# Block inverses with 32x32 weights in the RWKV part, and weights loaded in 512 KB halves

## The chip, the core and the metric

The kernel runs on one core of one Trainium2 chip. Its metric is the device time of one execution in microseconds (us), the median of three runs. It holds three transformer-like blocks behind one another, in float32, for 256 tokens of width 2048 (batch 1).

## The reference, cut to what matters

Nearly all arithmetic is the product of 256 tokens with large weight matrices. The part of the change that touches arithmetic lies in the first block, in the RWKV-7 mixer, whose recurrence over 256 positions is this (16 heads of 64):

```python
def step(state, inp):
    rt, wt, kt, vt, kkt, at = inp
    sa = jnp.einsum('bhvk,bhk->bhv', state, -kkt)
    state = (state * wt[:, :, None, :] + sa[..., None] * (kkt * at)[:, :, None, :]
             + vt[..., :, None] * kt[..., None, :])
    yt = jnp.einsum('bhvk,bhk->bhv', state, rt)
    return state, yt
...
_, y = lax.scan(step, state0, seq_major)
```

The projections around it are plain products, the three blocks run one behind the other:

```python
h = _rms_norm(x, pre_norm_g[l])
proj = h @ w_in[l]
...
merged = (jax.nn.sigmoid(m_r + b_merge[l, 0]) * u_r + jax.nn.sigmoid(m_a + b_merge[l, 1]) * u_a)
x = x + _rms_norm(merged @ w_out[l], post_norm_g[l])
```

## The kernel before, in words

**The bulk.** All weight matrices are streamed once from HBM, in units of 1 MB (128 partitions x 8 chunks x 256 columns of float32), into `ring`, a ring of three units (`RING = 3`). Half a unit is a slot (`SLOT = 4` chunks). ScalarE rounds a slot to its high part (`split_high`, L2700), VectorE computes the low part (`split_low`, L2707), and TensorE multiplies: high weights with both parts of the tokens (L2847, 512 columns move) and low weights with the high part of the tokens (L2851, 256 columns move), 8 products of each in a slot. One slot takes about 3 us, and there are 1084 slots. The parts of the weights lie in four buffers (`PARTS = 4`), so ScalarE and VectorE can be two slots ahead.

**The loads.** SyncE issues them in `load_unit`: for unit u it waits until `low_split` has counted both slots of unit u - 3, then issues one DMA of 1 MB, whose landing is counted by `unit_loaded[u % 3]`. Only the very first unit is loaded in two halves. ScalarE waits for the whole unit before it splits its first slot.

**The side work.** Norms, attention, the recurrence and so on are threads: generators for each engine that yield places on the axis of slots. Each engine walks along the slots and runs whatever of a thread is due before the next piece of bulk work. The places are written by hand, partly in a table `MOVED`, and every engine executes in order. So each engine's sequence is fixed when the program is built.

**The inverse.** The recurrence is computed in chunks of 64 positions, four at a time for a pair of heads. There are four rounds (i = 0 to 3), and in each round two such pairs, here called the even and the odd one (`rw` in the code; the even one's tiles lie in `high`, the odd one's partly in `low`). Every chunk needs the inverse of a triangular 64x64 matrix. It is built by doubling: `x0` is the inverse of the diagonal blocks of 2, and level l (1 to 5) joins the diagonal blocks of width 2^l to blocks of twice the width. `xx[:, 0]` and `xx[:, 1]` hold the inverse so far and its transpose, `al` the part of the matrix that level l needs (POOL masks it, L1086). A level has two steps on TensorE:

- step y: 8 products for each pair, with weights from `al` and 32 moving columns from `xx`. ScalarE then copies the result to `yb` (L1241).
- step xx: 16 products for each pair (8 in level 5), with weights from `xx` and `yb`, after ScalarE's copy. VectorE then adds the result to `xx` (L1165, L1169).

The two heads of a pair sit on partitions 0 to 63 and 64 to 127, and so every product uses a 64x64 quarter of the array. Every float32 product shows in the trace as two loads of weights and two matmuls. All these products have the line of the helper `mm` (L1285), and they go by their tiles: `sidep` is where they write.

In the program TensorE has, for each level, step y of the even pair, step y of the odd pair, then step xx of both. In 12 of the 16 levels 2 to 5 (four rounds of four levels) no bulk product stands between y and xx; in the other four (levels 2, 4 and 5 of round 0, level 4 of round 2) 8 or more bulk products do.

Of the kernel before, what the change touches and what calls it, by code (L numbers as in the profile page):

```python
# [22 lines left out]
RING = 3  # L23
# [170 lines left out]
def build_kernel(nc, I, out_dram):  # L194
    ctx = ExitStack()
    with ctx:
# [3 lines left out]
        def sem(name):  # L200
            return ctx.enter_context(nc.semaphore(name))
# [4 lines left out]
        ring = sb("ring", [P, RING, UNIT, NB])  # L206
# [18 lines left out]
        gp = ctx.enter_context(nc.psum_tensor("gp", [P, 2, 2, 2, TOK], F32))  # L225
        sp_ = ctx.enter_context(nc.psum_tensor("sidep", [P, 4, 512], F32))

        unit_loaded = [sem(f"unit_loaded_{k}") for k in range(RING)]
        high_split, low_split, slot_used = sem("high_split"), sem("low_split"), sem("slot_used")
        lo_copied, block_evacuated = sem("lo_copied"), sem("block_evacuated")  # L230
        scaled_by_vector, scaled_by_pool = sem("scaled_by_vector"), sem("scaled_by_pool")
# [46 lines left out]
        S, order = {}, []  # L278
# [37 lines left out]
        n_slots = order[-1].end  # L316
        where = [(s, b, n) for s in order for b in range(s.blocks) for n in range(s.slots)]
# [37 lines left out]
        rows, row_list = {}, []  # L355
# [509 lines left out]
        v1 = high[:, 4096:6144].rearrange("p (t c) -> p t c", t=2)  # L865
# [121 lines left out]
        def block_columns(a, l, u):  # L987

            return a.rearrange("p c (b u w) -> p c b u w", u=2, w=1 << l)[:, :, :, u, :]
# [290 lines left out]
        def rwkv_tensor(pe):  # L1280
            HS = [slice(0, 64), slice(64, 128)]
            ACROSS = [(HS[0], HS[1]), (HS[1], HS[0])]

            def mm(out, lhs, rhs, start=True, stop=True):
                return pe.matmul(out, lhs, rhs, start=start, stop=stop, skip_group_check=True)  # L1285

            def crossed(rw, n):

                return HS[n ^ rw.th], HS[n]
# [16 lines left out]
            for i in range(4):  # L1306
# [9 lines left out]
                for rw in rwkv:  # L1316
# [5 lines left out]
                    for t in range(2):  # L1322
                        m = mm(rw.x[:, t * P:(t + 1) * P], t1[0:65, t * P:(t + 1) * P], w2p[0:65, j * P:(j + 1) * P])
# [57 lines left out]
                for l in range(1, 6):  # L1381
                    t = t0 + 14 + 4 * (l - 1)
                    yield t
                    for rw in rwkv:
                        if l == 1:
                            rw.ac.wait(pe, "bonus", i)
                        rw.po.wait(pe, f"al{l}", i)
                        rw.dv.wait(pe, "x0" if l == 1 else f"xx{l - 1}", i)
                        for c in range(4):
                            for s, o in ACROSS:  # L1390
                                m = mm(rw.x[o, c * 32:(c + 1) * 32], rw.al[s, l % 2, c, :], block_columns(rw.xx[s, 1], l, 0)[:, c])
                        rw.pe_.did(m, f"y{l}")
                    yield t + 2
                    for rw in rwkv:
                        rw.ac.wait(pe, f"y{l}", i)
                        for c in range(4):
                            if l < 5:
                                for s, o in ACROSS:
                                    mm(rw.yk[s, c * 32:(c + 1) * 32], rw.xx[o, 0, c, :], block_columns(rw.yb[o], l, 0)[:, c])
                            for s, o in ACROSS:  # L1400
                                m = mm(rw.x[o, 256 + c * 32:256 + (c + 1) * 32], rw.yb[o, c, :], block_columns(rw.xx[o, 0], l, 1)[:, c])
                        rw.pe_.did(m, f"xx{l}")
                for c in range(4):
                    t = t0 + 34 + 6 * c
# [1255 lines left out]

        loads_of_unit = []
        for u in range(n_slots // 2):
            s, b, n = where[2 * u]
            loads_of_unit.append((loads_of_unit[u - RING] if u >= RING else 0) + 16 * len(s.source(b, n // 2)))

        def load_unit(sp, u):
            s, b, n = where[2 * u]
            if u >= RING:  # L2670
                sp.wait_ge(low_split, 2 * (u - RING) + 2)
            for src, c0, width in s.source(b, n // 2):
                to = ring[:, u % RING].rearrange("p (c x) n -> p c (x n)", x=2) if s.wide else ring[:, u % RING, :, c0:c0 + width]
                sp.dma_start(to, src).then_inc(unit_loaded[u % RING], 16)

        first_half_loaded = sem("first_half_loaded")

        def load_half(sp, half):
            (src, _, _), = S["v1"].source(0, 0)
            to = ring[:, 0].rearrange("p (c x) n -> p c (x n)", x=2)  # L2680
            return sp.dma_start(to[:, 2 * half:2 * half + 2], src[:, 2 * half:2 * half + 2])

        def load_first_half(sp):
            load_half(sp, 0).then_inc(first_half_loaded, 16)

        def load_second_half(sp):
            load_half(sp, 1).then_inc(unit_loaded[0], 16)

        def split_high(act, q):
            if q >= n_slots:  # L2690
                return
            s, b, n = where[q]
            u = q // 2
            if q == 0:
                act.wait_ge(first_half_loaded, 16)
            else:
                act.wait_ge(unit_loaded[u % RING], loads_of_unit[u])
            if q >= PARTS:
                act.wait_ge(slot_used, q - PARTS + 1)
            act.activation(w_parts[:, q % PARTS, 0], ring[:, u % RING, SLOT * (q % 2):SLOT * (q % 2) + SLOT, :], ACT.Copy).then_inc(high_split, 1)  # L2700
# [241 lines left out]
```

## Time and profile before

| | |
|---|---|
| median of three runs | 3282.01 us (3281.84 to 3282.38) |
| the profiled execution | 3281.76 us, of which 3280.0 us span |
| TensorE busy (matmuls) | 3260.6 us, 99% of the span |
| weight loads of TensorE | 2829.2 us, 86% |
| VectorE, ScalarE, GpSimd | 2131.2, 1510.4, 359.0 us |
| granted TensorE clock | 0.999 |
| DMA | 181 GB/s in the mean, 55.3% of the 16 engines' span for the weights' queue |

How to read it: the span runs from the first to the last instruction; the execution's own time has 1.8 us around it. Busy time counts an engine's instructions. Matmuls overlap, so that TensorE's pace is read better from the distance between the starts of its instructions. The rows further down give a start, a length, an engine, the line of the kernel, out<-in by the names of the program, the shape, and how many instructions are merged into the row. A gap before an instruction is given in brackets with what ended it.

### The profile page before, as it was taken

Reading aid. Unit: us, or ns where it says so; the run is one execution under the profiler, and the core shown is the slowest. Engines: PE = TensorE matmul, PEld = TensorE weight load, DVE = VectorE, ACT = ScalarE, POOL = GpSimd, SP = SyncE. Lnnn points to the kernel's source line nnn. Section 1 sums busy time; section 2 is a strip of 40 time slices with the busy share of each in tenths; the row PEclk is TensorE's granted clock in tenths of the full one; section 3 lists DMA queues with packets and bytes.
Section 4 is the critical chain, followed back from the end, with each engine's and each line's share of the span. In section 5 each row is a group of like instructions: output and inputs, shape, how many; then the busy total and the mean of one; then the engine's idle time right before and its main releaser. Section 6 shows DMA issues by size and latency. Waiting matters only on the chain.

```text
span 3280.0 us, 50954 instructions
## 1 busy us (share of the span) xinstructions
PE 3260.6 (99%) x21299; PEld 2829.2 (86%) x21299; DVE 2131.2 (65%) x2795; ACT 1510.4 (46%) x2049; POOL 359.0 (11%) x356
## 2 busy tenths in 40 slices
PE   9999999999999999999999999999999999999999
PEld 8888888888878888888888888888888888888887
DVE  6468666567487677776765556656778765456654
ACT  5355434444544455445444444444455544334443
POOL 3000233310102004211000000012000100000000
PEclk9999999999999999999999999999999999999999
DMA  7455434456546456555556556555555555556554
GB/s 252 148 181 179 146 128 131 133 171 225 182 145 204 161 180 231 169 180 194 190 182 204 189 177 198 194 171 197 182 171 168 190 186 201 193 182 197 197 193 154
DMA packets 533065, 594.98 MB, mean 181 GB/s; under 512 B 16773, under 2 KB 475365, under 8 KB 532326
## 3 DMA queue, kind: packets, MB, share of 16 engines
q1 hardware_dynamic: 532694, 591.48, 55.3%
q8 instruction: 169, 2.77, 0.3%
q14 instruction: 58, 0.48, 0.0%
q10 hardware_dynamic: 144, 0.26, 0.0%
HBM read 585.32 MB, written 6.32 MB: 180 GB/s over the span
## 4 chain that ended last, share of the span: by engine, by line
PE 97%; DVE 2%; ACT 0%; POOL 0%; issue 0%; DMA 0%; SPq 0%; POOLq 0%; ACTq 0%; DVEq 0%
PE gp L2847 49%; PE gp L2851 26%; PE gp L2767 10%; PE gp L2773 5%; PE sidep L1285 3%; DVE w_parts L2707 1%; PE sidep L1571 0%; PE sidep L1575 0%; PE sidep L1853 0%; DMA high<-x 0%; PE sidep L1991 0%; PE sidep L833 0%; PE sidep L834 0%; DVE x_parts L2550 0%; PE sidep L960 0%
## 5 line engine op out<-in xcount | busy, mean ns | idle before, releaser
L2707 DVE TENSOR_TENSOR w_parts<-ring,w_parts 128x1024 fp32r<-128x1024 f32 x1084 | 1369.7, 1286 | 384.2 <-ACT w_parts L2700 382.0
L2700 ACT ACTIVATE w_parts<-ring 128x1024 fp32r<-128x1024 f32 x1084 | 1108.9, 1052 | 460.8 <-PE gp L2773 230.0
L2847 PE MATMUL gp<-x_parts,w_parts 128*128 128x512 f32 x5264 | 1296.6, 394 | 0.0
L2847 PEld LDWEIGHTS gp<-x_parts,w_parts 128*128 128x128 f32 x5264 | 958.9, 188 | 186.1 <-issue 2.5
L2851 PEld LDWEIGHTS gp<-x_parts,w_parts 128*128 128x128 f32 x5264 | 684.2, 191 | 34.5 <-issue 2.5
L2851 PE MATMUL gp<-x_parts,w_parts 128*128 128x256 f32 x5264 | 706.2, 284 | 0.4 <-DVE w_parts L2707 0.4
L2243 ACT ACTIVATE lo_half<-gp 128x512 f32<-128x512 f32 x220 | 131.6, 598 | 726.6 <-PE gp L2847 593.7
L2847 PE MATMUL gp<-ff_parts,w_parts 128*128 128x512 f32 x1792 | 430.4, 391 | 0.0
L2847 PEld LDWEIGHTS gp<-ff_parts,w_parts 128*128 128x128 f32 x1792 | 328.9, 188 | 63.3
L2372 DVE TENSOR_TENSOR stage<-gp,lo_half 128x512 f32<-128x512 f32 x168 | 116.0, 690 | 311.7 <-ACT lo_half L2243 309.7
L2767 PE MATMUL gp<-w_parts,ff_parts 128*128 128x512 f32 x1024 | 273.7, 389 | 0.0
L2851 PEld LDWEIGHTS gp<-ff_parts,w_parts 128*128 128x128 f32 x1792 | 231.1, 191 | 10.4 <-issue 1.0
L2851 PE MATMUL gp<-ff_parts,w_parts 128*128 128x256 f32 x1792 | 235.9, 283 | 0.0
L2767 PEld LDWEIGHTS gp<-w_parts,ff_parts 128*128 128x128 f32 x1024 | 192.2, 188 | 39.8
L658 POOL TENSOR_TENSOR low<-low 128x512 f32<-128x512 f32 (+1 forms) x38 | 59.7, 1577 | 1126.0 <-ACT low L649 655.3
L2773 PE MATMUL gp<-w_parts,ff_parts 128*128 128x512 f32 x512 | 157.6, 389 | 0.0
L2767 PE MATMUL gp<-w_parts,x_parts 128*128 128x512 f32 x512 | 140.4, 396 | 0.2 <-ACT w_parts L2700 0.2
L2259 ACT ACTIVATE ff_parts<-stage 128x512 fp32r<-128x512 f32 x64 | 40.5, 632 | 166.9 <-DVE stage L2409 166.9
L2773 PEld LDWEIGHTS gp<-w_parts,ff_parts 128*128 128x128 f32 x512 | 96.1, 188 | 20.0
L2767 PEld LDWEIGHTS gp<-w_parts,x_parts 128*128 128x128 f32 x512 | 94.8, 188 | 20.0 <-issue 0.4
L2372 DVE TENSOR_TENSOR high<-gp,lo_half 128x512 f32<-128x512 f32 x45 | 31.1, 690 | 109.9 <-ACT lo_half L2243 109.9
L2291 POOL TENSOR_TENSOR high<-high,rstd 128x512 f32<-128x512 f32 x26 | 46.6, 1796 | 340.2 <-DVE high L2372 340.2
(376 smaller groups left out, 2007.9 us busy)
## 6 DMA issues: line engine op xcount, KB each, us to landing
ring<-w_in SPq DMA_DIRECT2D x219, 1024.0 KB, 5.1
ring<-w_ff SPq DMA_DIRECT2D x128, 1024.0 KB, 5.6
ring<-w_up SPq DMA_DIRECT2D x64, 1024.0 KB, 5.8
ring<-w_down SPq DMA_DIRECT2D x64, 1024.0 KB, 4.9
ring<-w_out SPq DMA_DIRECT2D x48, 1024.0 KB, 5.5
ring<-w_branch_attn SPq DMA_DIRECT2D x8, 1024.0 KB, 6.0
ring<-w_branch_rwkv SPq DMA_DIRECT2D x8, 1024.0 KB, 5.7
gate_scratch<-stage SPq DMA_DIRECT2D x16, 256.0 KB, 2.2
```

Source lines behind the costliest of these rows:

```text
L658: m = pool.tensor_tensor(self.acc[k], self.acc[k], self.sq[b - 1][k], ALU.add)
L1285: return pe.matmul(out, lhs, rhs, start=start, stop=stop, skip_group_check=True)
L2243: act.activation(lo_half[:, k % 2], gp[:, k % 2, :, 1, :], ACT.Copy).then_inc(lo_copied, 1)
L2259: act.activation(ff_parts[:, 2 * b:2 * b + 2, 0, :], st, ACT.Copy).then_inc(ff_high_split, 1)
L2291: pool.tensor_tensor(to, to, over(rstd, 2), ALU.mult).then_inc(scaled_by_pool, 1)
L2372: v.tensor_tensor(to, gp[:, k % 2, :, 0, :], lo_half[:, k % 2], ALU.add).then_inc(block_evacuated, 1)
L2700: act.activation(w_parts[:, q % PARTS, 0], ring[:, u % RING, SLOT * (q % 2):SLOT * (q % 2) + SLOT, :], ACT.Copy).then_inc(high_split, 1)
L2707: v.tensor_tensor(w_parts[:, q % PARTS, 1], ring[:, u % RING, SLOT * (q % 2):SLOT * (q % 2) + SLOT, :], w_parts[:, q % PARTS, 0].bitcast(F ...
L2767: pe.matmul(wide_sums(k, t), operand(s, b, s.chunks * n + c)[:, half, tokens], w[:, 0, c, :], start=(n == 0 and c == 0 and half == 0), sto ...
L2773: m = pe.matmul(wide_sums(k, t), operand(s, b, s.chunks * n + c)[:, 0, tokens], w[:, 1, c, :], start=False, stop=(n == s.slots - 1 and c = ...
L2847: return pe.matmul(gp[:, k % 2, j, :, :], w_parts[:, q % PARTS, 0, c, j * P:(j + 1) * P], operand(s, b, SLOT * n + c), start=(n == 0 and c ...
L2851: return pe.matmul(gp[:, k % 2, j, 0, :], w_parts[:, q % PARTS, 1, c, j * P:(j + 1) * P], operand(s, b, SLOT * n + c)[:, 0, :], start=Fals ...
```

## The change

Four things are edited.

1. In levels 2 to 4, step y works on 32x32 blocks: for each chunk and each head two products with 32x32 weights and 16 moving columns instead of one with 64x64 weights and 32 moving columns. Level 1 is as before.
2. In level 5, step y has products with 32x32 weights (one quarter of `al`) and 32 moving columns, as many products as before.
3. In level 5, step xx does the same with a quarter of `yb` as weights.
4. Every unit is loaded by two DMAs of 512 KB, one for each slot. The first waits until `low_split` has counted one slot of unit u - 3, the second until it has counted both. Each half has its own semaphore for each place of the ring, and ScalarE waits for the half that it splits.

```diff
-                            for s, o in ACROSS:
-                                m = mm(rw.x[o, c * 32:(c + 1) * 32], rw.al[s, l % 2, c, :], block_columns(rw.xx[s, 1], l, 0)[:, c])
+                            if l == 1:
+                                for s, o in ACROSS:
+                                    m = mm(rw.x[o, c * 32:(c + 1) * 32], rw.al[s, l % 2, c, :], block_columns(rw.xx[s, 1], l, 0)[:, c])
+                            elif l < 5:
+                                for b in range(2):
+                                    for s, o in ACROSS:
+                                        m = mm(rw.x[half(o, b), c * 32 + b * 16:c * 32 + (b + 1) * 16],
+                                               rw.al[half(s, b), l % 2, c, b * 32:(b + 1) * 32],
+                                               block_columns(rw.xx[half(s, b), 1, :, b * 32:(b + 1) * 32], l, 0)[:, c])
+                            else:
+                                for s, o in ACROSS:
+                                    m = mm(rw.x[half(o, 1), c * 32:(c + 1) * 32], rw.al[half(s, 0), l % 2, c, 32:64],
+                                           rw.xx[half(s, 0), 1, c, 0:32])
...
-                                m = mm(rw.x[o, 256 + c * 32:256 + (c + 1) * 32], rw.yb[o, c, :], block_columns(rw.xx[o, 0], l, 1)[:, c])
+                                if l < 5:
+                                    m = mm(rw.x[o, 256 + c * 32:256 + (c + 1) * 32], rw.yb[o, c, :], block_columns(rw.xx[o, 0], l, 1)[:, c])
+                                else:
+                                    m = mm(rw.x[half(o, 0), 256 + c * 32:256 + (c + 1) * 32], rw.yb[half(o, 1), c, 0:32],
+                                           rw.xx[half(o, 1), 0, c, 32:64])
...
-            if u >= RING:
-                sp.wait_ge(low_split, 2 * (u - RING) + 2)
-            for src, c0, width in s.source(b, n // 2):
-                to = ring[:, u % RING].rearrange("p (c x) n -> p c (x n)", x=2) if s.wide else ring[:, u % RING, :, c0:c0 + width]
-                sp.dma_start(to, src).then_inc(unit_loaded[u % RING], 16)
+        def load_half(sp, u, half):
...
+            rows = slice(half * s.chunks, (half + 1) * s.chunks)
+            if u >= RING:
+                sp.wait_ge(low_split, 2 * (u - RING) + 1 + half)
+            sp.dma_start(to[:, rows], src[:, rows]).then_inc(half_loaded[u % RING][half], 16)
...
-            if q == 0:
-                act.wait_ge(first_half_loaded, 16)
-            else:
-                act.wait_ge(unit_loaded[u % RING], loads_of_unit[u])
+            act.wait_ge(half_loaded[u % RING][q % 2], 16 * (u // RING + 1))
```

On TensorE, in round 0, the products of level 3 with what stands around them, before (the first row is bulk; 64x32 means 64 partitions and 32 moving columns):

```order
L2851 MATMUL gp<-x_parts,w_parts 128x256 x8
L1285 MATMUL sidep<-high 64x32 x8
L1285 MATMUL sidep<-low 64x32 x8
L1285 MATMUL sidep<-high 64x32 x16
L1285 MATMUL sidep<-high,low 64x32 x2
L1285 MATMUL sidep<-low,high 64x32 x2
```

and the same place of the changed kernel (its L2859 is L2851 of before):

```order
L2859 MATMUL gp<-x_parts,w_parts 128x256 x8
L1285 MATMUL sidep<-high 32x16 x16
L1285 MATMUL sidep<-low 32x16 x16
L1285 MATMUL sidep<-high 64x32 x16
L1285 MATMUL sidep<-high,low 64x32 x2
L1285 MATMUL sidep<-low,high 64x32 x2
```

The two y rows have twice the products, each a quarter as large in weights; the xx rows and all places are the same.

On SyncE, the first loads of the ring and the loads behind the parameters, before:

```order
L2674 DMA ring<-w_in 128x4x512
L431 DMA high<-x 128x2x1024
L2674 DMA ring<-w_in 128x4x512
...
L2674 DMA ring<-w_in 128x4x512 x5
L2674 DMA ring<-w_in 128x8x256 x2
```

and of the changed kernel:

```order
L2688 DMA ring<-w_in 128x2x512 x2
L431 DMA high<-x 128x2x1024
L2688 DMA ring<-w_in 128x2x512 x2
...
L2688 DMA ring<-w_in 128x2x512 x10
L2688 DMA ring<-w_in 128x4x256 x4
```

Every load of a unit has become two with half the rows, at the same place of the queue; no other DMA has moved past one.

## Rows read from the trace of the kernel before

**Rows 1.** The page: busy time by engine (instructions), the last chain by engine.

```profile
PE 3260.6 (99%) x21299; PEld 2829.2 (86%) x21299; DVE 2131.2 (65%) x2795; ACT 1510.4 (46%) x2049; POOL 359.0 (11%) x356
...
PE 97%; DVE 2%; ACT 0%; POOL 0%; issue 0%; DMA 0%; SPq 0%; POOLq 0%; ACTq 0%; DVEq 0%
```

**Rows 2.** Busy time by stretch: stretch, length, PE, PEld, DVE, ACT, POOL, clock, DMA, GB/s.

```profile
460.00:540.00 80.00, 78.85 (x1223) 67.28 (x1222) 48.03 (x94) 31.52 (x61) 29.14 (x27) 1.00 0.39 127
```

**Rows 3.** Groups by form, 380 to 710 us: count, busy us, mean ns, idle before.

```profile
L1285 PEld LDWEIGHTS sidep<-high 64*64 64x64 f32 x1696 | 46.3, 134 | 19.7 <-issue 12.7 <-DVE high L1188 1.6 <-DVE high L1145 0.4
L1285 PE MATMUL sidep<-high 64*64 64x32 f32 x896 | 26.5, 222 | 0.0
...
L1285 PEld LDWEIGHTS sidep<-headones,high 128*128 128x128 f32 x56 | 6.8, 191 | 0.8 <-ACT high L1257 0.6
```

**Rows 4.** Order of time on PE, round 1, level 3, nothing between y and xx.

```profile
491.31 0.66 PE L1285 MATMUL sidep<-high 64*64 64x32 f32 x16
491.79 0.63 PE L1285 MATMUL sidep<-low 64*64 64x32 f32 x16
492.34 0.67 PE L1285 MATMUL sidep<-high 64*64 64x32 f32 x32
...
493.25 0.23 PE L1285 MATMUL sidep<-low,high 64*64 64x32 f32 x2
493.40 2.11 PE L2847 MATMUL gp<-x_parts,w_parts 128*128 128x512 f32 x8
```

**Rows 5.** Order of time on ScalarE at the same place.

```profile
492.01 0.28 ACT L1241 ACTIVATE high<-sidep 128x128 f32<-128x128 f32 x1 [3.41 <-PE sidep L1285]
492.48 0.28 ACT L1241 ACTIVATE high<-sidep 128x128 f32<-128x128 f32 x1 [0.19 <-PE sidep L1285]
```

**Rows 6.** PE, round 0, level 2, where bulk stands behind y.

```profile
405.04 0.66 PE L1285 MATMUL sidep<-high 64*64 64x32 f32 x16
405.52 0.63 PE L1285 MATMUL sidep<-low 64*64 64x32 f32 x16
406.09 2.11 PE L2847 MATMUL gp<-x_parts,w_parts 128*128 128x512 f32 x8
```

**Rows 7.** PE, round 1, level 5.

```profile
504.28 0.65 PE L1285 MATMUL sidep<-high 64*64 64x32 f32 x16
504.76 0.63 PE L1285 MATMUL sidep<-low 64*64 64x32 f32 x16
505.31 0.66 PE L1285 MATMUL sidep<-high 64*64 64x32 f32 x16
505.80 0.63 PE L1285 MATMUL sidep<-low,high 64*64 64x32 f32 x16
506.36 0.97 PE L2847 MATMUL gp<-x_parts,w_parts 128*128 128x512 f32 x3
```

**Rows 8.** PE, round 1, level 2, the second y step.

```profile
485.83 0.28 PE L1285 MATMUL sidep<-low 64*64 64x32 f32 x3
486.78 0.48 PE L1285 MATMUL sidep<-low 64*64 64x32 f32 x11 [0.68 <-issue]
```

**Rows 9.** The page's DMA queues: packets, MB, share.

```profile
q8 instruction: 169, 2.77, 0.3%
```

**Rows 10.** ScalarE's waits for loads, in all: us, times, longest.

```profile
ACT w_parts L2700 <- DMA ring<-w_in: 3.2, 3, 1.8
ACT w_parts L2700 <- DMA ring<-w_ff: 2.2, 1, 2.2
ACT w_parts L2700 <- DMA ring<-w_branch_rwkv: 2.2, 1, 2.2
```

**Rows 11.** TensorE's waits at the same splits, and SyncE's for a free place.

```profile
PE gp L2767 <- ACT w_parts L2700: 0.2, 1, 0.2
...
SPq L2674 <- DVE w_parts L2707: 2830.7, 528, 19.6
```

**Rows 12.** Loads of the ring from `w_in`: count, KB, median us to landing.

```profile
ring<-w_in SPq DMA_DIRECT2D x219, 1024.0 KB, 5.1
```

More of the change, by code:

```diff
@@ L226, in build_kernel @@
         sp_ = ctx.enter_context(nc.psum_tensor("sidep", [P, 4, 512], F32))
-        unit_loaded = [sem(f"unit_loaded_{k}") for k in range(RING)]
+        half_loaded = [[sem(f"half_loaded_{k}_{half}") for half in range(2)] for k in range(RING)]
         high_split, low_split, slot_used = sem("high_split"), sem("low_split"), sem("slot_used")
@@ L1285, in mm, with half @@
                 return pe.matmul(out, lhs, rhs, start=start, stop=stop, skip_group_check=True)
+            def half(s, b):
+                return slice(s.start + 32 * b, s.start + 32 * b + 32)
             def crossed(rw, n):
@@ L2658, in operand @@
             return x_parts[:, c]
-        loads_of_unit = []
-        for u in range(n_slots // 2):
+        def load_half(sp, u, half):
             s, b, n = where[2 * u]
-            loads_of_unit.append((loads_of_unit[u - RING] if u >= RING else 0) + 16 * len(s.source(b, n // 2)))
-        def load_unit(sp, u):
-            s, b, n = where[2 * u]
-            if u >= RING:
-                sp.wait_ge(low_split, 2 * (u - RING) + 2)
-            for src, c0, width in s.source(b, n // 2):
-                to = ring[:, u % RING].rearrange("p (c x) n -> p c (x n)", x=2) if s.wide else ring[:, u % RING, :, c0:c0 + width]
-                sp.dma_start(to, src).then_inc(unit_loaded[u % RING], 16)
[L2676 to L2681, printed above, removed]
+            (src, c0, width), = s.source(b, n // 2)
+            to = ring[:, u % RING].rearrange("p (c x) n -> p c (x n)", x=2) if s.wide else ring[:, u % RING, :, c0:c0 + width]
+            rows = slice(half * s.chunks, (half + 1) * s.chunks)
+            if u >= RING:
+                sp.wait_ge(low_split, 2 * (u - RING) + 1 + half)
+            sp.dma_start(to[:, rows], src[:, rows]).then_inc(half_loaded[u % RING][half], 16)
+        def load_unit(sp, u):
+            load_half(sp, u, 0)
+            load_half(sp, u, 1)
         def load_first_half(sp):
-            load_half(sp, 0).then_inc(first_half_loaded, 16)
+            load_half(sp, 0, 0)
         def load_second_half(sp):
-            load_half(sp, 1).then_inc(unit_loaded[0], 16)
+            load_half(sp, 0, 1)
         def split_high(act, q):
```

## The prediction

> **What bounds the kernel now.** I read the page first. TensorE is busy for 3260.6 of 3280.0 us, its clock stays at the full level, and the last chain of waits is 97% TensorE [rows 1]. So time is won or lost only where TensorE's own stream becomes shorter or where TensorE stands still. The view by stretches then shows the part that holds the inverse, 380 to 700 us: TensorE has some 1220 matmuls in 80 us there, VectorE and ScalarE stand at 48 and 32 us of 80, and DMA at 0.39 [rows 2]. No other engine is near its limit in it. The groups by form show what is to be changed: 896 matmuls of 64x32 in one of four such groups, 1792 in all (112 products of levels 1 to 5 for each pair and round, 8 pairs and rounds, two records each), and weight loads of 64 columns with 134 ns against 191 ns with 128 columns [rows 3]. Last I read the order of time at single levels, since busy time of overlapping matmuls says little.
>
> **What one step costs.** In a step y 16 records take 0.48 us (491.31 to 491.79), and they go through two quarters of the array at once: 8 turns of 60 ns. In a step xx 64 records of both pairs take 1.06 us (492.34 to 493.40), of which 0.15 us is the change back to the whole array, so about 15 ns each: four quarters at once, again in turns of 60 ns [rows 4]. The length of a turn is thus set by one quarter's load of weights and matmul, not by how many quarters run. A load of 64 fewer columns is 57 ns shorter [rows 3], 0.89 ns for a column. With 32 columns a turn should be 28 ns shorter, and 8 turns 0.23 us. Since the first turn has a start-up that stays, I take 0.215 us for each changed step. Level 2 to 4 have twice the records in y, but four tiles of the array instead of two, and so 8 turns as well.
>
> The trace has no 32x32 product, so this has two ends. From below: a turn stays at 60 ns, and nothing is won. From above: it falls to what four records need if only their starting counts. The densest row has 15 ns for a record [rows 4], but that is a turn of 60 ns shared by four; it does not show that 15 ns is the least. I take 32 ns for a turn, as the weight loads of two widths lie on a line. I keep both ends.
>
> **The sum, part by part.**
>
> (a) Levels 2 to 4 without bulk between y and xx: 9 of them (of the 12 such levels, 3 are level 5). Here ScalarE's copy decides when xx may start. The even y begins at 491.31, ScalarE's copy at 492.01 and ends at 492.29, xx begins at 492.34, 1.03 us after y [rows 4, 5]. TensorE's own work before xx, two steps y, will be 0.27 + 0.25 us, but the copy can come earlier only by what the even y becomes shorter. So xx starts at about 0.85 instead of 1.03 us, 0.18 us are won, and the rest of what y saves becomes a wait of TensorE. The odd pair's copy is ready at about 1.12, before xx of the even pair is through. 9 x 0.18 = 1.6 us.
>
> (b) Levels 2 to 4 with bulk behind y (3): y of both pairs was 0.48 + 0.57 us [rows 6], and the copy is hidden by the bulk. Both savings count: 3 x 0.43 = 1.3 us.
>
> (c) Level 5 without bulk between (3): 504.28 to 506.36 is 2.08 us [rows 7]. Now xx even starts at 0.85 and takes 0.27; the odd copy follows the even one (start 0.52, each 0.28 us [rows 5]) and lets xx odd start at 1.12; it then takes 0.56 - 0.215 = 0.35. End at 1.47: 3 x 0.6 = 1.8 us.
>
> (d) Level 5 with bulk between (1): four steps, 4 x 0.215 = 0.9 us.
>
> (e) The change between ways of dividing the array. From 64x64 back to the whole array it costs 0.15 us from the last start to the next (493.25 to 493.40) where a turn is 0.06 [rows 4]. The change adds none where y or level 5 borders on bulk. It adds one of 32x32 to 64x64 in each of the 9 levels of (a), between odd y (through at about 0.54) and xx (0.85): it lies inside the wait for the copy. I take 0; without that cover it is at most 9 x 0.15 = 1.35 us. The Trainium skill says the same more strictly (TensorEngine Tiling, Key Properties): changing the mode of tiling drains the engine, changing the tile does not. The trace agrees with its 0.15 us; by that rule with nothing hidden the sum would be 1.35 us smaller.
>
> (f) The gap at 485.9. In the odd y of level 2, round 1, the records stop for 0.95 us from the start of one row to the next, where three records take 0.09, with no semaphore waited for ("issue") [rows 8]. The page has a DMA queue that loads instructions, 169 packets with 2.77 MB, some 16 KB each [rows 9]; with 42,598 loads and matmuls [rows 1] that is about 65 bytes for an instruction, and 250 in a packet. My reading: TensorE had used up its instructions and waited 0.86 us for the next packet. Such a packet shares the DMA engines with a weight load, which is under way for 5.1 us of every 6 [rows 12]. Halves make these bursts shorter, and all positions move. I count 0.86 x 0.7 = 0.6 us as won.
>
> (g) The halves themselves. The first half of a unit may start one slot (3 us) earlier, and a half lands sooner. But in the whole program ScalarE waited only 7.6 us for a load in five places [rows 10], and TensorE 0.2 us for such a split [rows 11]: the two slots of lead cover the rest. SyncE waits 2830.7 us for places of the ring [rows 11], so 542 more issues (about 0.4 us each) lie in idle time. Behind the added wait for the first slot stands the wait for the second, which ends when it ended before, so no store or side load comes later. I take 0. The bounds: +0.3 us if some side load is late, -0.5 if the first units help.
>
> Sum: 1.6 + 1.3 + 1.8 + 0.9 + 0.6 = 6.2 us. 3281.76 - 6.2 = 3275.6 for an execution like the profiled one, which lies 0.25 us under the median of the runs: **3275.8 us**.
>
> Nothing else is uncovered by it: between xx of a level and y of the next stands bulk of 1 to 3 us, in which VectorE adds and POOL masks, and these move together with TensorE's stream.
>
> **The rivals.**
>
> *B, four 32x32 tiles do not run together.* For it: the trace never has more than two row groups, and no record pace under 15 ns [rows 4]. Against: the pairs of a turn start together, and xx runs four quarters. Then 32 records of y need 0.48 us as the 32 of an xx do, and (a) and (b) are worth nothing, while level 5 (two tiles at a time) keeps (c) and (d): 2.7 + 0.6 = 3.3 us, 3278.7. The Trainium skill has a rule for this (TensorEngine Tiling, Gotcha 1: PSUM Pressure): row tiles cannot write one bank of PSUM at the same time. All tiles of a step y write one bank. The trace does not bear it out for two row tiles, whose matmuls in y go in pairs.
>
> *C, a 32-column load is not shorter.* Then no step changes its time, and what remains is the 32-to-64 change, partly behind the copy: 9 x 0.08 (0.15 less the wait of 0.07 that is there now) = 0.7 slower: 3282.7. For it: nothing under 64 columns is in the trace. Against: the line through 134 and 191 ns.
>
> *D, slower: TensorE runs out of instructions more often.* The place is the run of y and xx: a level of (a) has 192 instructions in 2.1 us now and 256 in 1.9 us afterwards, a whole packet. Each gap costs 0.86 us [rows 8]. There was one in 16 levels. It takes 7 new ones to use up the 5.6 us of (a) to (d), from 8 on the kernel is slower; 14 would make it 3288. For it: the existing gap lies in just such a run. Against: one in 16, and shorter bursts of weight loads.
>
> *E, more is won:* steps and copies become shorter by what 32 rows and 16 columns save in a matmul's 219 to 222 ns [rows 3], 0.03 us in each of 16 levels and 12 copies, 0.8 us, and the gap of (f) goes for good: 3274.5.
>
> **How the numbers follow.** Forecast 0.58 (its own range 3275.0 to 3277.2), B 0.18, C 0.07, D 0.05, E 0.12. The range of 8 in 10 takes in E and B and leaves C and D out: 3274.2 to 3279.8. A difference of 0.2% is 6.6 us, about the least that a measurement of this kernel can tell from no change; that is 3275.4. E and somewhat under half of the forecast's share lie beyond it: faster 0.38, within 0.2% 0.57, slower 0.05 (D).
>
> **What the profile would show.** 32x32 weight loads of about 106 ns; in level 3 of round 1 0.27 us from even to odd y and xx 0.85 us after y, with a wait of TensorE for ScalarE before it; level 5 in 1.47 us; the row of 485.9 without its gap; bulk rows with the same pace. The forecast is wrong if the even y still takes 0.48 us (B or C), if rows with "issue" gaps multiply (D), or if the bulk's pace or TensorE's waits for `w_parts` move (g).

## The result: slower by 0.25%, not faster

| | before | after |
|---|---|---|
| median (range), 9 runs each | 3281.65 us (3280.59 to 3282.38) | **3289.87 us** (3285.02 to 3293.58) |
| the profiled execution, its span | 3281.76, 3280.0 us | 3288.11, 3286.4 us |
| mean granted clock | 0.999 | 0.997 |

The ratio is 1.0025 [1.0016, 1.0033]. The forecast was 3275.8 us with a range of 3274.2 to 3279.8, and 0.05 for slower: it was wrong, in sign too. The runs of after also scatter over 8.6 us, those of before over 1.8.

**The steps that were changed.** They came out as forecast. The groups by form of after, 380 to 710 us (columns as in [rows 3]):

```profile
L1285 PEld LDWEIGHTS sidep<-high 32*32 32x32 f32 x512 | 7.1, 112 | 4.3 <-issue 1.0 <-ACT high L1241 0.8 <-POOL high L1090 0.7
L1285 PE MATMUL sidep<-high 32*32 32x16 f32 x384 | 5.7, 186 | 0.0
```

A weight load of 32 columns takes 112 ns, where 64 take 134. Now TensorE in round 1, level 3, which answers to [rows 4]:

```profile
494.09 0.44 PE L1285 MATMUL sidep<-high 32*32 32x16 f32 x32
494.37 0.52 PE L1285 MATMUL sidep<-low 32*32 32x16 f32 x32
494.94 0.67 PE L1285 MATMUL sidep<-high 64*64 64x32 f32 x32
...
496.01 0.73 PE L2855 MATMUL gp<-x_parts,w_parts 128*128 128x512 f32 x2
```

and ScalarE there, which answers to [rows 5] (both copies merged into one row):

```profile
494.61 0.62 ACT L1241 ACTIVATE high<-sidep 128x128 f32<-128x128 f32 x2 [3.25 <-PE sidep L1285]
```

The even y takes 0.28 us for 32 matmuls (0.48 for 16 before), and xx starts 0.85 us after y instead of 1.03. Level 2 of round 0, with bulk behind y, answers to [rows 6]:

```profile
405.30 0.44 PE L1285 MATMUL sidep<-high 32*32 32x16 f32 x32
405.57 0.45 PE L1285 MATMUL sidep<-low 32*32 32x16 f32 x32
405.95 1.42 PE L2855 MATMUL gp<-x_parts,w_parts 128*128 128x512 f32 x5
```

0.65 us instead of 1.05. And level 5 of round 1, which answers to [rows 7]:

```profile
507.52 0.44 PE L1285 MATMUL sidep<-high 32*32 32x32 f32 x16
507.79 0.42 PE L1285 MATMUL sidep<-low 32*32 32x32 f32 x16
508.44 0.44 PE L1285 MATMUL sidep<-high 32*32 32x32 f32 x16 [0.23 <-ACT high L1241]
508.71 0.42 PE L1285 MATMUL sidep<-low,high 32*32 32x32 f32 x16
509.06 2.11 PE L2855 MATMUL gp<-x_parts,w_parts 128*128 128x512 f32 x8
```

1.54 us instead of 2.08 here, 1.44 in the other two.

**Where the time went.** TensorE's waits in after, whole program (engine, tile and line, releaser: total us, times, longest):

```profile
PE sidep L1285 <- issue: 5.6, 4, 1.8
...
PE gp L2855 <- issue: 0.5, 1, 0.5
```

An "issue" wait is one that nothing in the trace ends. Before had one of 0.7 us [rows 8]. The longest two, in TensorE's order of time (round 0, level 3, and round 3, level 2):

```profile
411.62 0.22 PE L1285 MATMUL sidep<-low,high 64*64 64x32 f32 x1
413.51 0.24 PE L1285 MATMUL sidep<-low,high 64*64 64x32 f32 x1 [1.67 <-issue]
...
414.10 2.08 PE L2855 MATMUL gp<-x_parts,w_parts 128*128 128x512 f32 x4
...
662.13 0.28 PE L1285 MATMUL sidep<-high,low 64*64 64x32 f32 x3
664.19 0.19 PE L1285 MATMUL sidep<-high,low 64*64 64x32 f32 x1 [1.78 <-issue]
```

In the middle of a step xx, whose line the change does not touch, TensorE stands still for 1.89 us from start to start, and nothing that it waits for is in the trace. The five gaps are, from start to start: 1.89 (411.6), 0.73 (489.1), 1.05 (503.7), 1.82 (579.5) and 2.00 us (662.2), 7.5 in all. The one at 489.1 is in the same step as the gap of before, the odd y of level 2, round 1:

```profile
488.90 0.34 PE L1285 MATMUL sidep<-low 32*32 32x16 f32 x19
489.79 0.30 PE L1285 MATMUL sidep<-low 32*32 32x16 f32 x13 [0.56 <-issue]
```

So the old gap did not go, and four came with the change.

The bulk row at 414.10 shows a second loss: four products take as long as eight do [rows 4]. The view by stretches, around the gaps (columns as in [rows 2]):

```profile
405.00:411.60 6.60, 6.48 (x247) 5.43 (x248) 2.15 (x5) 3.04 (x8) 2.26 (x4) 1.00 0.57 183
411.60:413.50 1.90, 0.23 (x16) 0.12 (x8) 0.55 (x2) 0.64 (x1) 0.59 (x1) 1.00 0.86 250
413.50:420.00 6.50, 6.49 (x134) 4.71 (x134) 1.68 (x3) 0.94 (x3) 0.00 (x0) 0.54 0.35 110
...
581.30:588.10 6.80, 6.80 (x139) 5.43 (x138) 1.70 (x5) 1.04 (x3) 3.40 (x4) 0.50 0.46 138
...
664.20:670.00 5.80, 5.68 (x152) 4.94 (x152) 2.22 (x6) 2.05 (x5) 2.64 (x4) 1.00 0.02 6
```

Before, during and behind the gap the granted clock is 1.00, 1.00 and 0.54: after 1.9 us with TensorE at 0.23 us busy it fell to its lower level of 1.2 GHz. The trace's clock records give 6.83 us at 0.5 here and again from 581.27, behind the gap of 579. Behind the gap of 662, which is longer, it stayed at 1.00. The Trainium skill has idle time of TensorE as the cause of such a fall (TensorE: Matmul & The Clock Gate, Part 1: The HAM clock gate); the rows at 411 and 579 agree, the one at 662 shows that the length of one gap does not settle it.

**The balance of the two spans.** Steps: 9 x 0.18 + 3 x 0.4 + 1.8 + 0.9 = 5.5 us won. New gaps: 7.5 less the 5 x 0.06 us that such records take anyway, less the old one, 0.86: +6.3. Clock: at half speed four products of 512 columns take 2.01 us from start to start (414.10 to 416.11) instead of 1.12 (412.43 to 413.55 in before), and a step y or xx about 1.5 to 1.7 times its time, so 6.83 us cost about 2.9: twice, +5.8. Sum +6.6; the spans differ by 6.4 (3286.4 - 3280.0).

**What the gaps have in common.** I numbered the records of TensorE in the trace, that is its entries: weight loads, matmuls and its own semaphore and drain entries. The 16 profiles have 39 such gaps, all between 400 and 670 us. In every one the first record behind it has the number 193 over a multiple of 256, and the packet of the instruction queue that began last before it is always the same one: with packets counted from 0, record 256k + 449 follows packet k. The page of after, answering to [rows 9]:

```profile
q8 instruction: 172, 2.82, 0.4%
```

So the instructions come in packets of 256 (16 KB of 64 bytes each), and the boundaries stand at fixed numbers. That gives the theory for the experiments: TensorE asks for a packet some 294 records before it needs it (near record 155 over a multiple of 256, by the packets that begin soonest), the packet begins 0.1 to 6.4 us later (after, 380 to 710 us), and its instructions can be used about 2.35 us after it began (2.2 to 2.8 over the 39 gaps; 411.10 to 413.51 in after, 484.35 to 486.78 before). Where 294 records take longer than both, nothing is seen. In bulk alone, with 32 records in a slot of 3 us, they take some 27 us. In a level without bulk 256 records take 1.9 us.

### The profile page after: what moved, and what is told of

The parts are those of the page before. It is cut to its first block, busy times and chain, and to the rows that moved or that the text cites. A ratio compares the mean times of both kernels' runs of the same rounds, so it can differ in the third digit from the quotient of the medians.

```text
span 3286.4 us, 52263 instructions
## 1 busy us (share of the span) xinstructions
PE 3260.2 (99%) x21683; PEld 2826.8 (86%) x21683; DVE 2131.5 (65%) x2795; ACT 1511.0 (46%) x2049; POOL 358.5 (11%) x356
## 3 DMA queue, kind: packets, MB, share of 16 engines
q8 instruction: 172, 2.82, 0.4%
## 4 chain that ended last, share of the span: by engine, by line
PE 96%; DVE 2%; ACT 1%; issue 1%; POOL 0%; DMA 0%; SPq 0%; POOLq 0%; ACTq 0%; DVEq 0%
PE gp L2855 49%; PE gp L2859 25%; PE gp L2775 10%; PE gp L2781 5%; PE sidep L1285 3%; DVE w_parts L2715 1%; PE sidep L1589 0%; PE sidep L1593 0%; DMA high<-x 0%; PE sidep L1871 0%; PE sidep L2009 0%; PE sidep L833 0%; PE sidep L834 0%; DVE x_parts L2568 0%; PE sidep L960 0%
## 5 line engine op out<-in xcount | busy, mean ns | idle before, releaser
L2859 PEld LDWEIGHTS gp<-x_parts,w_parts 128*128 128x128 f32 x5264 | 684.3, 191 | 34.4 <-issue 2.5
L2859 PE MATMUL gp<-x_parts,w_parts 128*128 128x256 f32 x5264 | 706.2, 284 | 0.4 <-DVE w_parts L2715 0.4
L2859 PEld LDWEIGHTS gp<-ff_parts,w_parts 128*128 128x128 f32 x1792 | 231.0, 191 | 10.4 <-issue 1.0
L2859 PE MATMUL gp<-ff_parts,w_parts 128*128 128x256 f32 x1792 | 235.9, 283 | 0.1
```

Source lines behind the costliest of these rows:

```text
L2859: return pe.matmul(gp[:, k % 2, j, 0, :], w_parts[:, q % PARTS, 1, c, j * P:(j + 1) * P], operand(s, b, SLOT * n + c)[:, 0, :], start=Fals ...
```

## The experiments

Sixteen levels have many chances to meet a boundary, and one added record moves all later ones. All runs below are timed in five rounds against before on the same chip (fill_192 and fill_256 on another chip than the rest); the medians of before were 3281.3 to 3281.6 us. The intervals of the ratios are about 0.1% (3 us) to either side, so that no time alone decides between runs less far apart; there the gaps in the traces have to carry the reading. "Gaps" are TensorE's "issue" gaps, from start to start, in the profiled execution; "half clock" is the time at 0.5 in its clock records, between 380 and 710 us.

| run | median (range) us | ratio to before | span | gaps, us | half clock |
|---|---|---|---|---|---|
| inverse_only | 3290.86 (3289.55-3295.28) | 1.0030 [1.0019, 1.0042] | 3292.7 | 2.82 0.99 2.37 3.37 | 23.9 |
| halves_only | 3280.98 (3280.28-3282.07) | 0.9998 [0.9989, 1.0007] | 3279.9 | 0.62 | 0 |
| level5_only | 3278.88 (3278.28-3279.39) | 0.9991 [0.9982, 1.0] | 3277.4 | 1.10 | 0 |
| level5_halves | 3278.78 (3277.95-3279.62) | 0.9990 [0.9982, 0.9999] | 3277.3 | 0.82 | 0 |
| one_block | 3276.32 (3275.20-3277.73) | 0.9985 [0.9977, 0.9994] | 3274.6 | 0.57 1.11 | 0 |
| twice_64 | 3296.42 (3296.03-3297.72) | 1.0047 [1.0033, 1.006] | 3294.7 | 0.59 0.77 1.50 | 3.4 |
| more_records | 3286.43 (3285.26-3289.64) | 1.0015 [1.0007, 1.0024] | 3285.8 | 0.43 2.77 | 6.8 |
| level5_fill | 3278.61 (3278.15-3279.00) | 0.9991 [0.9983, 1.0] | 3277.0 | 0.46 | 0 |
| even_only | 3285.41 (3282.96-3289.76) | 1.0014 [1.0005, 1.0023] | 3283.5 | 0.81 0.40 0.42 1.99 1.62 1.12 | 3.4 |
| split_only | 3286.30 (3281.60-3288.05) | 1.0012 [1.0003, 1.0021] | 3283.1 | 0.82 2.25 2.13 0.56 | 3.4 |
| change_fill | 3283.78 (3283.13-3286.07) | 1.0009 [1.0, 1.0017] | 3282.0 | 0.95 0.48 1.59 2.16 | 6.8 |
| even_fill | 3291.00 (3284.74-3293.00) | 1.0028 [1.0018, 1.0038] | 3290.3 | 2.14 2.22 | 23.9 |
| fill_192 | 3283.62 (3283.23-3284.87) | 1.0007 [0.9998, 1.0016] | 3281.8 | 1.02 | 0 |
| fill_256 | 3283.04 (3282.32-3283.75) | 1.0005 [0.9996, 1.0013] | 3281.4 | 0.88 | 0 |

### Which edit costs

**inverse_only** is the change with whole loads of 1 MB, **halves_only** the loads in halves with the inverse of before.

> The 32x32 products of levels 2 to 5 with whole 1 MB loads. Theory S (the denser bursts of instructions run TensorE out of instructions, whatever the loads are): three or more gaps without a semaphore in the levels of the inverse, the level steps themselves as short as in the changed kernel (y to xx 0.85 us, level 5 in 1.44 us), and a time of 3283 to 3292 us that varies by several us from run to run. Theory H (the halves delay the instruction packets, the products alone are harmless): at most one gap and 3275 to 3277 us, with runs within 1 us of each other.

> Only the loads in halves, the inverse with 64x64 products as before. Theory S: no more gaps than before (one, or none), 3281 to 3283 us. Theory H: two or more gaps and 3284 us or more, since two or three loads of 512 KB are now under way at once and an instruction packet waits behind them.

The loss is all with the inverse; the halves alone are within 0.03% of before (just under what was expected), and their one gap is that of before: theory H, that the halves delay the packets, is refuted. Without the halves the gaps are even longer, up to this one in TensorE's order of time:

```profile
665.54 0.28 PE L1285 MATMUL sidep<-high,low 64*64 64x32 f32 x3
668.96 0.19 PE L1285 MATMUL sidep<-high,low 64*64 64x32 f32 x1 [3.15 <-issue]
```

**level5_only** has the small products in level 5 alone, **level5_halves** also the halves. Neither adds a record. The edit against the change:

```diff
-                            if l == 1:
+                            if l < 5:
                                 for s, o in ACROSS:
                                     m = mm(rw.x[o, c * 32:(c + 1) * 32], rw.al[s, l % 2, c, :], ...
-                            elif l < 5:
-                                for b in range(2):
...
```

> 32x32 products in level 5 alone, with whole loads; the number of instructions is that of before. By the steps measured in the changed kernel each of three level 5 becomes 0.64 us shorter (2.08 to 1.44) and one 0.8 us: 2.7 us less, 3279.0 us, if no gap is added. Theory S: it stays so, as no burst has more instructions, though level 5 runs through its 128 instructions in less time; with one new gap 3280 to 3283 us. Theory H says the same of this kernel.

> 32x32 products in level 5 alone, with the loads in halves. Theory S: as with level 5 and whole loads, 3278 to 3280 us. Theory H: two or more gaps, 3282 us or more. If both theories hold a part (bursts and late packets together), this one lies with level 5 and whole loads, and the full change is the worst of all.

Both hit: 2.7 us are won, as (c) and (d) had it. One gap is left, at the same product as before ([rows 8]), here in level5_only:

```profile
484.88 0.28 PE L1285 MATMUL sidep<-low 64*64 64x32 f32 x3
486.04 0.48 PE L1285 MATMUL sidep<-low 64*64 64x32 f32 x11 [0.88 <-issue]
```

### More records, or faster ones

**one_block** leaves out the second 32x32 block of step y in levels 2 to 4 (with whole loads); so it has the small products, but as many records as before. Against the change:

```diff
                             elif l < 5:
-                                for b in range(2):
+                                for b in range(1):
```

> The 32x32 products with whole loads, but in levels 2 to 4 step y computes only the first of its two 32x32 blocks (the other block is left out). The records are as many as before the change, and the steps as short as in the change. Theory S with the count of instructions as the cause: at most one gap, the clock at its full level all the time, and about 3276 us (3281.6 less the 5.6 us that the steps were to give). Theory S with the density as the cause (more instructions for a time, whatever their count): three or more gaps, 3282 us or more.

3276.3 us, 5.1 under before: the steps' 5.5 us, less 0.8 for a second gap, within 0.4. Small and fast products alone bring no new long gap; they do bring a second short one (0.57 us, where at most one was expected), at a boundary that before crossed without a stop: the same records come faster.

**twice_64** has the large products of before, each of levels 2 to 4 twice: the records of the change.

```diff
-                            for s, o in ACROSS:
+                            for s, o in ACROSS * (2 if 1 < l < 5 else 1):
                                 m = mm(rw.x[o, c * 32:(c + 1) * 32], ...
```

> The kernel before, with every 64x64 product of step y issued twice in levels 2 to 4: as many records as in the change, at the pace of before. Each of the 24 steps y takes 0.48 us more, 11.5 us in all, less nothing, so 3293 us without gaps. Count as the cause: gaps at 411, 490 and 580 us too, since a level now has 256 instructions, but shorter ones than in the change by about the 0.96 us that a level is longer: 3293 to 3297 us. Density as the cause: no new gap, 3292.5 to 3293.5 us.

In its interval, but the gaps stand at 413.7, 662.5 and 666.7 us, and not at 490 and 580 as expected. Here the reading by the median misleads: of the 14.7 us more span most is the second y itself, and the gaps are only 2.9 us, where the change has 7.5. It does not tell the number from the place.

**more_records** is before with 32 small identity products near the start (at 10 us, four records each), where TensorE waits for its first data; **level5_fill** the same with 16 of them on level5_halves.

```diff
+                if g == 2:
+                    fill(pe, 32)
                 pe.wait_ge(x_loaded[(0, 1, 2, 2, 3, 3, 3, 3)[g]], 16)
```

> The kernel before, with 32 small 64x64 products of the identity at the start, where TensorE waits for the tokens anyway: 128 more records, none of them in the inverse. Theory P (instructions come in packets of 256, a late packet stops TensorE at a record whose number is 193 over a multiple of 256): the gap at 485.9 us goes, and gaps appear at other places of the program, again at such a number. By the time from the request of a packet (155 records over a multiple) to the last record that TensorE has, the tightest places are at 487, 578 and 650 us (3.9 to 4.0 us, against over 5.6 everywhere before); one to three gaps there, 3282 to 3285 us. Theory Q (the gap at 485.9 is a matter of that place in the program, such as its data or its DMA): the gap stays at that step, no other, and 3281.6 to 3282.5 us.

> 32x32 products in level 5, loads in halves, and 16 small products at the start (64 records), so that the packet that is late at 485 us is requested before the denser step. Theory P: no gap at 485, the tightest places 4.8 us at 401 and 478 us, which is enough for a packet that starts 1 to 2 us after its request; 3278.8 less 0.8 = 3278.0 us. Theory Q: the gap stays, 3278.8 us or a little more.

The inverse of more_records is that of before to the last instruction, and its long gap comes 640 us later than the added products, which cost 0.8 us themselves (the first bulk behind them starts at 11.49 us, before at 10.68). Yet it is 5 us slower. In its order of time, round 3, a step xx that had no gap before:

```profile
651.69 0.23 PE L1293 MATMUL sidep<-high,low 64*64 64x32 f32 x2
654.46 0.32 PE L1293 MATMUL sidep<-low,high 64*64 64x32 f32 x2 [2.55 <-issue]
```

64 records ahead (level5_fill) cost nothing, 128 cost 5 us. I had expected the gaps of more_records at 487, 578 and 650 and 3282 to 3285. Those at 578 (0.43 us) and 652 came, the one at 487 did not, and the time is over the interval, as the clock fell behind the long gap (6.83 us), which no expectation had counted.

### Half of the change, and other places

**even_only** has the 32x32 blocks of levels 2 to 4 in the even pair alone, since only its y decides when ScalarE may copy; **split_only** in the three levels with bulk behind y; both have level 5 as in the change, and whole loads. Each of the two lines is the condition of one run, named behind it:

```diff
-                            if l == 1:
+                            if l == 1 or l < 5 and rw is rwkv[1]:                   # even_only
+                            if l < 5 and (i, l) not in ((0, 2), (0, 4), (2, 4)):    # split_only
```

> Only the even pair's y of levels 2 to 4 has 32x32 blocks (level 5 as in the change, whole loads). The even y alone decides when ScalarE's copy may start, so (a) should be kept whole (1.6 us) and half of (b) (0.65 us), with half of the added records (384 instead of 768). Theory N (it is the number of records of TensorE that comes too fast for the packets, and each added one counts): level5_only's 3278.9 less 2.2, plus one gap or two of 0.5 to 2 us in place of the four: 3277 to 3281, point 3279; a mark of the theory is that every gap stands where the record's number is 193 over a multiple of 256. Rival G (gaps come only where a whole packet of 256 lies in one level without bulk, which 224 records don't reach): no new gap, 3276.6.

> 32x32 blocks only in the three levels (round 0 levels 2 and 4, round 2 level 4) in which bulk products stand between y and xx, and level 5 as in the change, whole loads. Step (b) forecasts 1.3 us for these three: level5_only's 3278.9 less 1.3 = 3277.6. The 192 added records stand where bulk gives the packets time, so theory N expects no gap of their own (they move later boundaries by 64 to 192 records, which may cost or give back one gap of 0.5 to 1 us): 3277 to 3278.6. If the mere presence of 32x32 blocks brought the gaps, 2 us or more would be added: 3279.6 or more.

Both fall outside their intervals, and split_only falsifies what I then held: it adds 192 records where bulk is near, was to win 1.3 us, and lost 7.4 against level5_only. Its two longest gaps are in a step xx of round 0 and in bulk of round 1, neither of which it edits:

```profile
416.48 0.28 PE L1285 MATMUL sidep<-high,low 64*64 64x32 f32 x4
418.80 0.30 PE L1285 MATMUL sidep<-low,high 64*64 64x32 f32 x4 [2.03 <-issue]
...
493.91 0.73 PE L2865 MATMUL gp<-x_parts,w_parts 128*128 128x512 f32 x2
496.38 1.22 PE L2865 MATMUL gp<-x_parts,w_parts 128*128 128x512 f32 x2 [1.74 <-issue]
```

**change_fill** is the whole change with 24 small products ahead (96 records), **even_fill** even_only with 16.

> The whole change, and 24 small identity products before it all (96 records, under 1 us, where TensorE waits for the first loads anyway). All later records move by 96 against the boundaries of the packets. If a gap depends on where a boundary falls, the gaps at 411.6 and 662 should change their places or lengths: the boundaries then fall at about 410, 416, 491, 495, 579 and 661. The time lies anywhere between 3283 and 3292, but the profile's gaps stand at other products than in the change. The densest spots (491 and 579) lie in runs of more than 256 records, so that no shift frees the change of its gaps: at least two are left. If a gap belongs to a product (a tile, a mode of the array) and not to a boundary, places and time stay as they are, 3289.9.

> even_only with 16 small identity products before it all (64 records). Against even_only it tells how much the place of the boundaries does at half of the added records: theory N expects the same number of gaps give or take one, at other places, 3276.6 to 3281; rival G the same as even_only, 3276.6.

With the same inverse and loads, 96 records ahead make the change 6 us faster, as expected with gaps at other products; 64 ahead make even_only 5.6 us slower, 10 us over the interval, with two long gaps in place of six gaps, and 23.9 us at half clock. change_fill's first gap stands in y of the next level instead of in xx:

```profile
413.53 0.32 PE L1293 MATMUL sidep<-low 32*32 32x16 f32 x16
414.62 0.31 PE L1293 MATMUL sidep<-low 32*32 32x16 f32 x16 [0.77 <-issue]
```

No theory in which a record has a price explains both signs. Left is the place of the boundaries.

### The decisive pair

**fill_192** and **fill_256** are more_records with 48 and 64 products. 256 records bring every boundary back to its old product.

> The kernel before with 64 small identity products in front (256 records). Theory Z (what counts is where the boundaries of the packets of 256 records fall in the stretches without bulk, not how many records there are): 256 records bring every later boundary back to the product at which it stood before. The inverse then has the one gap of before, again in the odd y of level 2 of round 1, and none like the 2.8 us at 652 that 128 records brought. The products themselves delay the start: 128 of them took 0.8 us of TensorE's first bulk, 256 should take 2.0 us. So 3281.5 + 2.0 = 3283.5, 3282.5 to 3284. Rival C (each added record costs by its number): twice the loss of 128 records, 3281.5 + 10 = 3291.

> The same with 48 products (192 records), which cost 1.4 us at the start. Theory Z: the boundaries fall inside runs without bulk at about 487 and 578 (the 294 records from a packet's request to the first of the next take 4.1 to 4.2 us there, where 2.4 us and a packet's delay of 2 to 4 us are needed), so one or two gaps of 0.5 to 2 us at those places, each at a record whose number is 193 over a multiple of 256: 3281.5 - 0.8 + 1.4 + 1 to 5 = 3283 to 3287, point 3284.5. Rival C: between 128 and 256 records, 3289.

fill_256 hit: 3283.04, although it has twice the added records of more_records. The gap is back at its old product, after the third matmul of the odd y of level 2, round 1 ([rows 8]):

```profile
487.20 0.28 PE L1293 MATMUL sidep<-low 64*64 64x32 f32 x3
488.14 0.48 PE L1293 MATMUL sidep<-low 64*64 64x32 f32 x11 [0.66 <-issue]
```

The count up to it, by stretches, first in before and then in fill_256 (columns as in [rows 2]):

```profile
0.00:486.50 486.50, 481.00 (x3869) 414.84 (x3870) 317.37 (x499) 221.84 (x356) 90.51 (x128) 1.00 0.53 174
```

```profile
0.00:487.90 487.90, 483.39 (x3997) 417.60 (x3998) 317.28 (x499) 222.10 (x356) 90.49 (x128) 1.00 0.53 173
```

128 matmuls and 128 loads more, the same product, the same gap. fill_192 has its one gap at 577.9, one of the two places that the spacing of records had named, and its time is in the interval, 0.9 us under the point. That time has some luck in it: besides the gap of 1.02 us, TensorE waits 0.97 us at 967 us for a small side DMA, which no theory had named:

```profile
967.15 2.00 PE L1664 MATMUL sidep<-high 64*128 64x256 f32 x16 [0.97 <-DMA high<-high]
```

The pair also answers another rival, that the added products act by moving TensorE in time against the loads: fill_192 and more_records start the bulk at the same time (0.82 and 0.81 us later than before), and yet they have different gaps and times 2.8 us apart. (The fills cost less than I took: 1.35 us for 256 records, 0.82 for 192, by the start of the first bulk behind them.)

**What adds up and what doesn't.** Take before's span, less the steps (5.5, or the part of them that a run has), plus the start of the fill, plus gaps (less 0.06 each and the old 0.84), plus 0.42 us for each us at half clock (2.9 / 6.83). inverse_only: 3280.0 - 5.5 + 9.3 - 0.84 + 10.0 = 3293.0, measured 3292.7. more_records: 3280.0 + 0.8 + 3.1 - 0.84 + 2.9 = 3286.0, measured 3285.8. fill_256: 3280.0 + 1.35 + 0.82 - 0.84 = 3281.3, measured 3281.4. change_fill: 3280.0 - 5.5 + 0.7 + 4.9 - 0.84 + 2.9 = 3282.2, measured 3282.0 (the 0.7 is from the fills of 64 and 128 records, 0.57 and 0.8). In fill_192, split_only and even_only the sum is 0.9, 1.0 and 1.8 us too low. In fill_192 it is the wait for the side DMA shown above, in split_only the same wait (0.90 us at 968). In even_only 1.1 us of it are the steps themselves, which give less there. Round 2, level 2:

```profile
575.91 0.44 PE L1285 MATMUL sidep<-high 32*32 32x16 f32 x32
576.28 0.65 PE L1285 MATMUL sidep<-low 64*64 64x32 f32 x16
```

Where 64x64 products follow at once, the even y takes 0.37 us until the next start instead of 0.27: the change from 32x32 to 64x64 costs 0.10 us when no wait hides it. Each of the 12 levels then wins 0.09 us, where the expectation had 0.18 to 0.22. About 0.7 us stay unexplained.

The best versions with the whole computation are level5_fill and level5_halves, 3278.6 and 3278.8 us: 2.8 us, 0.09%, under before (the intervals end at 1.0000 and 0.9999), and 11 us under the change. Two runs that differ by so little are not told apart.

## Why the prediction was wrong

- **(a) to (d), right.** 0.18 us in a level without bulk, 0.40 of 0.43 with bulk, level 5 in 1.44 to 1.54 us for 1.47, and 0.84 of 0.86 in the level 5 of round 0. Medians confirm the sum: level5_only won 2.7 us of 2.7, one_block 5.1 of 5.6, and its second gap takes 0.8 of that.
- **Rivals B and C, refuted.** 32 matmuls in 0.28 us, in four tiles at once, and loads of 112 ns. The rule that the Trainium skill has on one bank of PSUM (TensorEngine Tiling, Gotcha 1: PSUM Pressure), and that B leaned on, does not show in either step y: each writes one bank, from two rows of tiles before and from four in the change, and its turns take 60 and 32 ns.
- **(e), right.** Between odd y and xx TensorE waits for ScalarE in any case, and xx starts at 0.85 us. The change of mode is hidden; even_only shows it uncovered, at 0.10 us, not 0.15.
- **(g), right.** halves_only: 0.9998. ScalarE waits 1.6 us for loads in after instead of 7.6, and TensorE gains nothing.
- **(f) and rival D: the steps that failed.** (f) read the gap of 485.9 rightly, as a packet of instructions that came late, and then treated it as an accident of 0.86 us that would probably go away, with 0.6 us counted as won. It stayed, in the same step, with 0.73 us in after and 0.62 in halves_only. It is no accident: at every boundary, one in 256 records, TensorE stops if the packet comes too late, and before happens to have its boundaries well placed: fill_192 and more_records, with the same inverse, show a gap of 1.0 us, and gaps of 0.4 and 2.8 us. D was the right mechanism with the wrong figures. Its price of 0.86 us a gap came from the only one that the trace had; measured were 0.4 to 3.4 us, 1.5 in the mean of after. Its "one in 16 levels" was a rate where a position was at work: 768 added records move the boundaries differently at each level. And it left out the clock, 5.8 of the 12 us lost. Not seven new gaps but four brought the change to a loss. A chance of 0.05 stood on one observation; "positions move" was in the text, as a reason for a gain.
- **What could have been read before.** The boundaries can be counted in the trace of before, and how long the 294 records ahead of each take. With the boundaries where they are, none between 380 and 710 us has less than 5.6 us for them; moved by 32 to 240 records, there is always one with 3.8 to 5 us, against 2.35 us and the delay of the packet. So before stands at one of the few good places, and nearly every shift is worse, though this does not tell by how much: its one gap came with 7 us for those records, from a packet delayed by 5.5 us.

**Open.** What delays a packet is not shown. In the whole of after the median delay is 1.0 us where fewer than 3 packets of weights are in flight in the first us behind the request, and 1.8 us where 14 or more are, but delays of over 6 us came in both cases. No run changed the loads alone at a bad place; inverse_only against after (whole loads and halves, gaps of 9.6 and 7.5 us) suggests that loads matter and shows no more than that. Why the clock fell behind 1.8 us at 579 and not behind 2.0 us at 662 is open too. Both probably make the runs of one kernel scatter, 8.6 us in after and 1.1 in level5_only. The table's gaps belong to one execution each, since each kernel has one profile.

## What to carry to other kernels

Count the records of the engine that bounds the kernel, not only their time: where many short products stand close together, the stream of instructions is a resource of its own, and adding or removing instructions anywhere ahead moves its boundaries. Before an edit that changes a count is judged, time it again with a few harmless instructions in front; if that alone moves the time by more than the edit, what was measured is the place. Prefer edits that keep the number of instructions, as level 5 here.

## What the hardware showed that I had not expected

- TensorE's instructions arrive 256 at a time; a late packet stops it for up to 3.4 us in the middle of a step, with no releaser in the trace, always at record 193 over a multiple of 256.
- 128 added records at 10 us bring a gap of 2.8 us at 652 us, and another 128 take it away.
- The granted clock fell to 0.5 during or soon after 13 of the 16 gaps of 1.5 to 3.4 us, for 3.4 to 17 us, and at none of the 23 shorter ones. It stayed at 1.00 with 2.00 us (after, 662), 2.25 us (split_only, 416) and 1.62 us (even_only, 580), so that the length of the gap does not decide it. At 0.42 us for each us at half clock a fall costs an estimated 1.4 to 7 us, in 7 of the 13 cases more than its gap (even_fill: 4.4 us of gaps, 23.9 us at half clock, some 10 us).
- Four 32x32 tiles run together at 32 ns a turn (494.146 to 494.178 to 494.210 in after), also where all write one bank of PSUM.
- Changing from 32x32 to 64x64 tiles costs 0.10 us where no wait hides it (even_only).
